# Turning three column groups of a residual on VectorE instead of TensorE, twice

## The reference

```python
h = h + y                                  # y = o @ nsa_w_out, the first output projection
hn = rms_norm(h, norm_ffn[i])
h = h + jnp.square(jax.nn.relu(hn @ ffn_w1[i])) @ ffn_w2[i]      # D_FF = 8192, in four chunks of 2048
gate = jax.nn.sigmoid(rms_norm(h, norm_ple[i]) @ ple_w_gate[i])
```

## Time and profile before

| what | value |
|---|---|
| time, median of 3 runs | 2210.76 us (2210.42 to 2211.42) |
| span of the profiled execution | 2209.0 us |
| around the span (median less span) | 1.8 us |
| busy: TensorE matmul / VectorE / ScalarE / GpSimd | 99% / 65% / 50% / 25% |
| 16 pieces of the projection (from 346.78) | ends at 393.05 us |
| down stage of the fourth chunk | from 1022.72 us |

### The profile page before, as it was taken

The page is one execution under the profiler, slowest core; times in us unless marked ns, Lnnn a source line. Parts: engine busy times, 40 slices in busy tenths (PEclk is TensorE's granted clock), DMA queues, the critical chain, the costliest instruction groups (busy, mean ns, idle before and its releaser), DMA issues.

```text
span 2209.0 us, 34195 instructions
## 1 busy us (share of the span) xinstructions
PE 2197.2 (99%) x11625; PEld 1878.9 (85%) x11625; DVE 1445.2 (65%) x1925; ACT 1106.9 (50%) x1654; POOL 550.7 (25%) x531
## 2 busy tenths in 40 slices
PE   9999999999999999999999999999999999999998
PEld 7888988888888888888888887888888888888887
DVE  6877765555664565555566667567785688756875
ACT  6445555453453454445455455565553455534553
POOL 3202220350240141053000033005540245403431
PEclk9999999999999999999999999999999999999999
DMA  7675335556555555556555653545555555555554
GB/s 254 232 230 163 115 128 204 170 190 208 191 190 192 189 189 192 186 192 193 187 185 179 227 171 135 193 160 188 195 188 196 192 183 192 189 195 192 186 209 149
DMA packets 118072, 414.21 MB, mean 188 GB/s; under 512 B 12896, under 2 KB 18048, under 8 KB 117472
## 3 DMA queue, kind: packets, MB, share of 16 engines
q1 hardware_dynamic: 111600, 401.37, 53.9%
q10 hardware_dynamic: 6384, 11.70, 1.7%
HBM read 409.29 MB, written 2.15 MB: 186 GB/s over the span
## 4 chain that ended last, share of the span: by engine, by line
PE 98%; DVE 1%; ACT 1%; issue 0%; DMA 0%; DVEq 0%; ACTq 0%
PE bank L486 33%; PE bank L494 17%; PE bank L543 7%; PE bank L545 7%; PE bank L544 7%; PE bank L1059 4%; PE bank L1060 4%; PE bank L1061 4%; PE bank L599 1%; PE bank L601 1%; PE bank L600 1%; PE bank L619 1%; PE bank L994 1%; PE bank L656 1%; PE bank L796 1%; PE bank L798 1%
## 5 line engine op out<-in xcount | busy, mean ns | idle before, releaser
L1100 DVE TENSOR_TENSOR wboth<-raw,wboth 128x1024 fp32r<-128x1024 f32 x756 | 982.2, 1302 | 607.8 <-ACT wboth L1802 607.1
L1802 ACT CAST wboth<-raw 128x1024 fp32r<-128x1024 f32 x756 | 790.9, 1049 | 711.5 <-PE bank L545 241.6
L486 PE MATMUL bank<-A,wboth 128*128 128x512 f32 x2928 | 705.1, 391 | 0.3 <-DVE wboth L1100 0.3
L486 PEld LDWEIGHTS bank<-A,wboth 128*128 128x128 f32 x2928 | 537.0, 188 | 104.6 <-issue 1.0
L494 PEld LDWEIGHTS bank<-A,wboth 128*128 128x128 f32 x2928 | 376.7, 191 | 14.8
L494 PE MATMUL bank<-A,wboth 128*128 128x256 f32 x2928 | 384.0, 283 | 0.0
L543 PE MATMUL bank<-wboth,H 128*128 128x512 f32 x576 | 224.6, 390 | 0.0
L545 PE MATMUL bank<-wboth,H 128*128 128x512 f32 x576 | 224.2, 389 | 0.0
L544 PE MATMUL bank<-wboth,H 128*128 128x512 f32 x576 | 224.1, 389 | 0.0
L2257 POOL TENSOR_TENSOR bias<-z,rs 128x256 f32<-128x256 f32 x64 | 75.7, 1182 | 481.2 <-DVE z L1131 391.6
L2257 POOL TENSOR_TENSOR PT<-z,rs 128x256 f32<-128x256 f32 x88 | 73.4, 835 | 465.4 <-DVE z L1131 464.8
(11 more groups left out here) (293 smaller groups left out, 2409.1 us busy)
## 6 DMA issues: line engine op xcount, KB each, us to landing
raw<-wstream SPq DMA_DIRECT2D x756, 512.0 KB, 3.3
bias<-bias_rows ACTq DMA_DIRECT2D x6, 512.0 KB, 5.4
x<-xrows ACTq DMA_DIRECT2D x1, 2048.0 KB, 10.0
bias<-grows ACTq DMA_DIRECT2D x2, 1024.0 KB, 6.1
out<-x SPq DMA_DIRECT2D x8, 256.0 KB, 2.1
x<-xT SPq DMA_DIRECT2D x7, 256.0 KB, 4.6
pA<-bias_rows ACTq DMA_DIRECT2D x2, 512.0 KB, 8.9
Sm<-grows ACTq DMA_DIRECT2D x1, 1024.0 KB, 5.8
```

Source lines behind the costliest of these rows:

```text
L486: last = nc.tensor.matmul(bank(j)[:, :], whi[:, s, cols(i)], moving(j, k), start=(k == 0), stop=(k == K - 1))
L1100: V.tensor_tensor(wlo[:, s, :], raw[:, s, :], whi[:, s, :].bitcast(F32), ALU.subtract).then_inc(lo_ready, 1)
L1802: C.copy(whi[:, s, :], raw[:, s, :]).then_inc(hi_ready, 1)
```

## The change

TensorE no longer turns groups 0, 1 and 2 of the two stages. VectorE does it with block transposes of 32 x 32: `turn_quarters` takes 32 token rows (of both token tiles) and for each quarter j of the 128 columns of all four tiles writes the transposed blocks into z, 32 partitions x 256 floats per instruction. Four instructions make one i, 16 a group; a group is done in two halves (i = 0, 1 and i = 2, 3) in two following steps of the stage. ScalarE's `turned_hi` and VectorE's `turned_lo` then read z instead of banks 4 to 7. `turned_hi` waits for the whole group (`4 * f + 4`), where `tiles_hi` waited tile by tile. Group 3 of both stages stays as it was.

```diff
             for f in range(2, 4):
-                rows_group(PB["wo"] + 8 * f, PB["wo"] + 8 * f, UB["wo"] + 2 * f, UB["wo"] + 2 * f, DT, H,
-                           between={2: lambda: turn_wo(2)} if f == 3 else {1: lambda: turn_wo(0), 4: lambda: turn_wo(1)})
+                rows_group(PB["wo"] + 8 * f, PB["wo"] + 8 * f, UB["wo"] + 2 * f, UB["wo"] + 2 * f, DT, H)
...
                     for f in range(4):
-                        down(f // 2, f % 2, between={2: lambda: turn_fd(f - 1)} if f else {})
+                        down(f // 2, f % 2)
...
+            def turn_quarters(f, i0, turned):
+                for i in (i0, i0 + 1):
+                    rows = xN[32 * i:32 * i + 32, :, f * WIDE:f * WIDE + WIDE].rearrange("p t (d c) -> p d t c", c=P)
+                    for j in range(4):
+                        cols = z[32 * j:32 * j + 32, :, :].rearrange("p d (t c) -> p d t c", t=QT)
+                        last = V.transpose(cols[:, :, :, 32 * i:32 * i + 32], rows[:, :, :, 32 * j:32 * j + 32])
+                    last.then_inc(turned, 1)
+            def turned_lo(dst, name, f, hi_sem, ready):
+                for d in range(4 * f, 4 * f + 4):
+                    dve.wait_ge(hi_sem, d + 1)
+                    V.scalar_tensor_tensor(dst[:, d, 1, :], z[:, d % 4, :], gain(name, d), dst[:, d, 0, :].bitcast(F32),
...
+            def wo_turn(f, i0):
+                if i0 == 0:
+                    dve.wait_ge(z_ready, 4 + UB["wo"] + 2 * f + 2)
+                if f == 0:
+                    dve.wait_ge(z_used, 4 + ZB["wo"])
+                elif i0 == 0:
+                    dve.wait_ge(a1_ready, 4 * f)
+                turn_quarters(f, i0, wo_turned)
...
             rows_body(PB["wo"] + 16, PB["wo"] + 16, 8, 2, lambda f: wo_in(f + 2),
-                      {3: lambda: wo_lo(0), 6: lambda: wo_lo(1), 12: lambda: wo_lo(2)})
+                      {0: lambda: wo_turn(0, 0), 1: lambda: wo_turn(0, 2), 3: lambda: wo_lo(0), 4: lambda: wo_turn(1, 0),
+                       5: lambda: wo_turn(1, 2), 6: lambda: wo_lo(1), 9: lambda: wo_turn(2, 0), 10: lambda: wo_turn(2, 2),
+                       12: lambda: wo_lo(2)})
...
+                    turns = {8 * f + 8 + i: lambda f=f, i=i: fd_turn(f, 2 * i) for f in range(3) for i in range(2)}
                     rows_body(PB[fd], PB[fd], 8, 4, lambda f: fd_in(f // 2, f % 2),
-                              {8 * f + 4: lambda f=f: fd_lo(f - 1) for f in range(1, 4)})
+                              {**turns, **{8 * f + 4: lambda f=f: fd_lo(f - 1) for f in range(1, 4)}})
...
+            def turned_hi(dst, name, f, turned, hi_sem):
+                act.wait_ge(turned, 4 * f + 4)
+                for d in range(4 * f, 4 * f + 4):
+                    C.activation(dst[:, d, 0, :], z[:, d % 4, :], ACT.Copy, scale=gain(name, d)).then_inc(hi_sem, 1)
```

More of the change, by code:

```diff
@@ L1217, in tiles_lo @@
                                            ALU.mult, ALU.subtract).then_inc(ready, 1)
+            def turn_quarters(f, i0, turned):
[9 more added lines that the diff above has]
+                    V.scalar_tensor_tensor(dst[:, d, 1, :], z[:, d % 4, :], gain(name, d), dst[:, d, 0, :].bitcast(F32),
+                                           ALU.mult, ALU.subtract).then_inc(ready, 1)
             def first_values():
@@ L1482, in _ @@
                         wo_in(f)
+            def wo_turn(f, i0):
[6 more added lines that the diff above has]
+                turn_quarters(f, i0, wo_turned)
             def wo_lo(f):
-                tiles_lo(A, "g_ffn", f, wo_hi, a1_ready)
+                if f < 3:
+                    turned_lo(A, "g_ffn", f, wo_hi, a1_ready)
+                else:
+                    tiles_lo(A, "g_ffn", f, wo_hi, a1_ready)
             rows_body(PB["wo"] + 16, PB["wo"] + 16, 8, 2, lambda f: wo_in(f + 2),
-                      {3: lambda: wo_lo(0), 6: lambda: wo_lo(1), 12: lambda: wo_lo(2)})
+                      {0: lambda: wo_turn(0, 0), 1: lambda: wo_turn(0, 2), 3: lambda: wo_lo(0), 4: lambda: wo_turn(1, 0),
+                       5: lambda: wo_turn(1, 2), 6: lambda: wo_lo(1), 9: lambda: wo_turn(2, 0), 10: lambda: wo_turn(2, 2),
+                       12: lambda: wo_lo(2)})
             def norm_ff():
@@ L1515, in chunk, with fd_turn @@
                         rows_body(o * 64 + it * 16 + PB[fd], PB[fd], 8, 2, lambda f: fd_in(it, f))
+            def fd_turn(f, i0):
+                if i0 == 0:
+                    dve.wait_ge(z_ready, 4 + UB["fd3"] + 2 * f + 2)
+                if f == 0:
+                    dve.wait_ge(z_used, 4 + ZB["fd3"])
+                elif i0 == 0:
+                    dve.wait_ge(a2_ready, 4 * f)
+                turn_quarters(f, i0, fd_turned)
             def fd_lo(f):
-                tiles_lo(A, "g_ple", f, fd_hi, a2_ready)
+                if f < 3:
+                    turned_lo(A, "g_ple", f, fd_hi, a2_ready)
+                else:
+                    tiles_lo(A, "g_ple", f, fd_hi, a2_ready)
             hidden(0, 0, mixed=1, between={1: lambda: wo_lo(3), 2: norm_ff, NORM_AT["ff0"]: lambda: take_rs(2, 0)})
@@ L1997, in wo_hi_of @@
             def wo_hi_of(f):
-                tiles_hi(A, "g_ffn", f, wo_turned, wo_hi)
+                if f < 3:
+                    turned_hi(A, "g_ffn", f, wo_turned, wo_hi)
+                else:
+                    tiles_hi(A, "g_ffn", f, wo_turned, wo_hi)
             rows_body(PB["wo"] + 16, PB["wo"] + 16, 0, 16, {
@@ L2031, in fd_hi_of @@
             def fd_hi_of(f):
-                tiles_hi(A, "g_ple", f, fd_turned, fd_hi)
+                if f < 3:
+                    turned_hi(A, "g_ple", f, fd_turned, fd_hi)
+                else:
+                    tiles_hi(A, "g_ple", f, fd_turned, fd_hi)
             hidden(0, 0, mixed=1, between={0: lambda: wo_squares(3), 1: lambda: wo_hi_of(3), 2: lambda: root(2, nrs, nvar)})
```

## The result

The changed kernel takes 2216.49 us (2216.01 to 2218.3, 11 runs) where the kernel before, in the same session, takes 2211.27 (2210.34 to 2212.1, 11 runs): 1.0025 times as long, with an interval of 1.0018 to 1.0033. That is 5.2 us more. Forecast were 3.5 us more, 2214.2 us, with a range of 2209 to 2221; so the time lies inside the range, and beyond the 0.2% that the forecast drew as the edge of "same".

What follows compares the result with a forecast made beforehand. TensorE bounds the kernel, busy 2197.2 of 2209.0 us. Projection 383.3 + 48p - 395.82, restarts +0.5, down stage -2.74 give 48p - 14.8, +3.5 us at p = 0.38: 2214.2 us, range 2209.0 to 2221.0.

Steps and rivals of the forecast that it cites:

- TensorE's saving: Both stages: six groups of TensorE transposes go, 0.91 us each, -5.5 us, all on the path.
- The price of a transpose: Both stages: each VectorE transpose of 32 partitions x 256 floats taken at 0.38 us, within 0.31 to 0.44.
- p: Time on VectorE from one block transpose to the next, 96 in all; bounds 0.20 to 0.60 us.
- the 0.395 row: Trace row of four VectorE scalar_tensor_tensor of 128x256, 0.395 us each, the only run of four of this size.
- the lone instruction's 476 ns: Trace row of one VectorE scalar_tensor_tensor of 128x256 that overlaps nothing: 0.476 us.
- full, unoverlapped instructions: Rival: VectorE transposes don't overlap, 0.45 to 0.48 us each, +6.8 to +8.3 us, 2217.6 to 2219; chance 0.18.
- The projection's chain: First output projection: VectorE's transposes delay pieces; the stage ends 5.7 us later instead of 2.7 earlier.
- h: From a group's last transpose through ScalarE's scaling and next rounding to that piece's split_lo on VectorE: 2.84 us.
- TensorE's restarts: Projection: some six restarts of TensorE after a wait, 0.08 us each, add 0.5 us.
- Every VectorE transpose of this stage is on the path from p = 0.21 on: Projection: group 3's transposes can start at 383.3 + 48p, before at 395.82; 48 transposes on the path.
- The down stage: Fourth down stage: VectorE's transposes hidden up to 0.52 us each, no TensorE wait, -2.74 us.
- The waits: Projection: TensorE waits before pieces 8, 9 (some 4 us at once), 13, 14 and group 3; none in the down stage.

Runs made afterwards that it cites:

- the down stage alone: Only the down stage uses VectorE's transposes, the projection as in the kernel before: 2208.11 us beside 2210.55, ratio 0.9988.
- The run with 20 instructions a group: Kernel with two of the projection's three groups on VectorE, plus four transposes per down-stage group into unused buffer PT: 2207.2 us, ratio 0.9982.
- the filled wait: Changed kernel plus 16 unread matmuls on TensorE between the projection's pieces 8 and 9: 2217.8 us, ratio 1.0031.
- the later scaling: Changed kernel, but in the projection ScalarE scales group 1 in step 7 instead of 5, low parts in step 8 instead of 6: 2213.1 us, ratio 1.0012.
- the second order: Changed kernel, projection reordered: group 1 turned right behind group 0, scaled in step 7; group 2 a step later: 2210.93 us, ratio 0.9998.

## Why the prediction was right, and where its size was off

- **TensorE's saving: right.** 0.91 us per group; the down stage alone gave 2.4 us (0.7 to 4.6 by its interval), 2.9 in its trace from the stage's start on, where 2.74 was forecast.
- **The price of a transpose: too low.** The step "I take p = 0.38, near the 0.395 row" failed. Measured is p = 0.4525, outside the stated 0.31 to 0.44, which the forecast itself had named as a sign of being wrong. The rate per element was right (1.04 ns measured, 1.05 forecast); the overlap failed. The 0.395 row is one of instructions that overlap; the transposes here change their source or target partitions each time and overlap nothing. Those that keep both, the ones to PT, follow in 0.37, the forecast's 0.38. The row that came close was the lone instruction's 476 ns, and the case that came true is the rival "full, unoverlapped instructions", priced at p of 0.45 to 0.48 and given a chance of 0.18. The Trainium skill, "VectorE: DVE Perf Modes", section "The three transpose paths", gave by the estimate in the prediction 0.45 us without overlap; the trace agrees in size (and 303 ns for 32x128 floats that overlap nothing stand beside the page's 311 for 128x128 in bf16). Of the rates of one and of two elements per cycle, which the prediction weighed by the Trainium skill, same page, section "The perf-mode tier table", the trace agrees with one, the case that the prediction put with its own 1.05 ns per element; two would have been half of that.
- **The projection's chain: right, and over-priced by about 1.2 us.** With the measured p the forecast's sum is 48 x 0.4525 - 14.8 = +6.9 us; measured are +5.3 in the span. Three terms make up the difference: (1) group 3 was put at 383.3 + 21.7 = 405.0, less the 0.34 by which the stage began earlier 404.7, and came at 403.93, 0.75 sooner. The part that the rows show is h, given as 2.84 and measured as 2.69 (from 370.32 + 8 x 0.4525 = 373.94 to 376.63): ScalarE starts 0.02 after the last transpose's slot and not 0.25. Over three groups that is some 0.45 us; the rest isn't taken apart. (2) The 0.5 us of TensorE's restarts doesn't add, since the path runs over VectorE while TensorE waits. (3) The 0.34 us of the earlier start.
- **"Every VectorE transpose of this stage is on the path from p = 0.21 on": right.** Half of them, as if p were 0.226, shorten the stretch by their whole 0.450 us each.
- **The down stage: right, its limit by luck.** At p = 0.4525 TensorE waits for nothing. The limit of 0.52 was worked out at the wrong piece: it set ScalarE's scaling, in h, ahead of `split_lo` 14, but in that step ScalarE rounds piece 14 first (at 1061.04) and scales then (1063.69), so h stands ahead of piece 15. What comes late first is piece 13, right behind the second half: 1047.03 + 16p + 1.25 + 1.33 = 1022.72 + 13 x 2.72 gives p = 0.53. That this is so near is chance: the forecast counted h (2.84) too much and allowed one piece (2.72) too much. The run with 20 instructions a group shows it: in 8.58 us, an equal p of 0.536, pieces 13, 21 and 29 are late, by 0.13 us, and no other.
- **The waits:** before pieces 8 and 9 and before group 3 as named, and before 14; the one "some 4 us at once" was 4.48. That before piece 13 didn't come: at the lower clock TensorE reached it later. The forecast said nothing of the clock; the filled wait shows that this costs no time.
- **Sign and time:** the forecast had the right sign, with a size of 0.16% that it called "same"; measured is slower by 0.25%. Only the size of p moves it across: 48 x (0.4525 - 0.38) = +3.5 us, less the 1.6 us of the point before, is about the 1.7 by which the forecast was low. That the time lies so near the forecast is in part luck: the error in p and those of the point before have opposite signs, and with p = 0.38 as forecast the others alone would have left some 1.8 us of slowdown.

## What to carry to other kernels

When work moves from the engine that sets the end to one with room, a full sum of free time says little; follow what is queued behind the new wait on each engine in between, here ScalarE's roundings behind its wait for a whole group. The same work cost nothing where eight pieces lay between two groups, and more than it saved where three groups fell into sixteen pieces; giving one of those back to TensorE, and scaling it two steps later, made 1.0025 into 0.998. For an instruction that no row shows, take the row of an instruction that overlaps nothing as a serious value, not as an outer case, and ask whether its source and target partitions are those of the instruction ahead of it.

## What the runs showed of the hardware

- VectorE's block transposes of 32x256 floats take 436 ns and follow each other every 0.4525 us, without the 0.08 us of overlap of other VectorE instructions, when the source or the target partitions change from one to the next. When both stay, the next starts 0.07 us before the end: after 0.37 us for 32x256 (12 instructions to PT), after 0.24 for 32x128 (96 pairs).
- Between 32x128 and 32x256, both without overlap, they cost 1.04 ns per element.
- The granted clock of TensorE fell to 0.50 after waits of 1.78 and 4.48 us; with the later scaling it fell as well, after waits of only 1.74 and 1.79. Windows of that kernel:

```profile
376.90:380.30 3.40, 3.40 (x10) 2.62 (x10) 3.40 (x7) 2.46 (x7) 0.00 (x0) 0.52 0.87 261
380.30:382.30 2.00, 2.00 (x10) 1.66 (x9) 1.99 (x4) 0.91 (x1) 0.00 (x0) 0.97 0.83 252
```

  With 1.73 and 0.91 in the filled kernel it didn't fall, and with 1.71 and 1.98 in the second order it didn't either (1.00 from 365 to 394), so the length of the waits alone doesn't tell. Where it fell, the stretch still ends with TensorE waiting for VectorE, 0.31 us in both kernels, which takes up the time lost.
